# Two seats of experts per round, each expert's weights kept while its blocks last, and tokens' rows scattered to DRAM before the experts run

## The chip, the cores and the metric

One Trainium2 chip, one core of it. The metric is the device time of one execution of the whole program in microseconds (us). The program is a stack of four fp32 layers of a language model for 512 tokens of width 1024. The change touches the mixture of experts of the last two layers.

## The reference

`reference` runs `first_block` (two layers of three mixers) and then `second_block` (two layers, `i` = 0 and 1). Each layer of the second block ends in a mixture of experts:

```python
N_EXPERTS, TOP_E, D_EXPERT = 32, 2, 512

def hier_moe(h, wr_g, br_g, wr_e, br_e, w_gate, w_up, w_down):
    xf = h.reshape(n_tok, d)                     # 512 tokens, d = 1024
    ...                                          # group by softmax, the 2 best experts in it
    gate = (p_top * jax.nn.softmax(e_val, axis=-1)).reshape(-1)
    expert_id = (g_sel * EXPERTS_PER_GROUP + e_sel).reshape(-1)
    ...
    def expert_block(args):
        xb, e = args                             # rows of tokens, their expert
        return (jax.nn.silu(xb @ w_gate[e]) * (xb @ w_up[e])) @ w_down[e]
    ...
    # a token's output is the gate-weighted sum over its two experts

x = x + g2[:, None, :] * hier_moe(h, ...)
```

The inputs are fixed, and so is the routing. Counted from the reference's own router on its own inputs, 1024 assignments fall on the 32 experts like this. Layer 0: experts 26 and 29 get 69 and 135 tokens, all the others between 2 and 61. Layer 1: expert 13 gets 67, all the others between 2 and 61. In blocks of 64 tokens that is 35 blocks in layer 0 (2 for expert 26, 3 for 29, 1 for each other) and 33 in layer 1 (2 for expert 13).

## The kernel before

Everything is fp32. Each layer of the second block ends in three stages, each a block of programs for the engines with a barrier behind it.

**route_and_plan** (`route`, `plan`). The vector engine (DVE) picks the two experts of each token. SyncE (SP) meanwhile issues the weights of experts 0 and 1, six loads. TensorE (PE) ranks each token within its expert by products with triangles and ones (L2569, L2570). DVE lays the work out as items: an item is one expert with up to 64 (`SLOTS`) of its tokens. Items 0 to 31 are the first block of each expert, the items behind them the further blocks. `slot_of` says for each token and item which slot it has, `row_of` where each token's two results will lie, `counts` holds the number of pairs of items and each item's expert. So layer 0 has 35 items in 18 pairs, layer 1 33 in 17.

**items** (`item_experts`). A loop over pairs of items, with a register as its bound. In pair `p` PE does

- gate: 16 products of `hs` with `wg`, two items side by side in the two halves of the array (L2701),
- up: the same with `wu`,
- gather of pair `p + 1` (L2693): `h` times a 0/1 matrix `pick` that DVE has made (L2753), 32 products, which give the turned rows of the next pair's tokens; ScalarE (ACT) copies them to `hs` (L2734) behind it,
- four transposes of `hid` (L2716), a copy to `hidT` on ACT (L2744), and down: 16 products with `wd` (L2701).

DVE multiplies `hid` (L2765) and scales the result `y` (L2772), GpSimd (POOL) stores it (L2678, 128x1024 fp32, 512 KB). SP reloads each of the three pairs of weight tiles as soon as PE is through with it (L2665, L2668, L2671): six loads of 2048 KB per pair, whichever expert stood there before. There is one buffer for each of the weight tiles, so a tile's load for pair `p + 1` lies between its use in `p` and in `p + 1`. In the trace a product of fp32 stands as two instructions.

**moe_residual**. POOL gathers each token's two rows from `expert_rows` by indirect DMA (L2819), DVE adds them to `x`. Rows of `expert_rows` that no token has are never read by a token, but they are cleared once: while the first block's layer 0 does its second attention (`attention` with `cleared_rows`), POOL issues 26 stores of zeros (L647, 13.6 MB). That attention reads its side weights `side_w` through SP's queue (L661). The same attention of the first block's layer 1 clears nothing.

Of the kernel before, what the change touches and what calls it, by code (L numbers as in the profile page):

```python
# [78 lines left out]
class Chip:  # L79
# [8 lines left out]
    def name_tables(self, t):  # L88
# [4 lines left out]
        self.before, self.block_starts, self.numbers, self.number = t["before"], t["block_starts"], t["numbers"], t["number"]  # L93
# [802 lines left out]
def first_layer(chip, l, io, par, row, x, fm, v_first, merged, o_fm, sg, next_norm):  # L896
# [3 lines left out]
    with ExitStack() as ctx:  # L900
# [5 lines left out]
        with ExitStack() as inner:  # L906
            def sbi(name, shape):
# [10 lines left out]
                  side=(fm, gate_jobs(fm, w_in, COL["gb"], sg)), cleared_rows=chip.expert_rows if l == 0 else None)  # L918
# [864 lines left out]
ITEMS = 2 * SEQ // SLOTS + EXPERTS + 4  # L1783
FAR = 16384.0
# [758 lines left out]
def plan(chip, st, choice, routed, routed_ready, slot_of, row_of, counts):  # L2543

# [6 lines left out]
    slot, t3 = st.sb("slot", [P, TILES, E]), st.sb("t3", [P, E, TILES * 2])  # L2551
    blocks, first = st.sb("blocks", [P, E]), st.sb("first", [P, E])
    last = st.sb("last", [P, E])
    slotT = st.sb("slotT", [E, SEQ])
    mine, rowf = st.sb("mine", [P, 2 * TILES, E]), st.sb("rowf", [P, 2 * TILES])
    rangeT, hot = st.sb("rangeT", [E, 2]), st.sb("hot", [E, ITEMS])
    row = st.sb("row", [1, 1 + ITEMS])
    half, over_one = st.sb("half", [1, ITEMS]), st.sb("over_one", [P, TILES, E])
    at_expert, later = st.sb("at_expert", [P, E]), st.sb("later", [E, ITEMS])
# [4 lines left out]
    @st.block.tensor  # L2564
    def _(pe):
        pe.wait_ge(*routed_ready.at(1))
        for t in range(TILES):
            product(pe, B[0][:, t * E:(t + 1) * E], [(chip.before, routed[:, t, :])] +
                    [(chip.ones, routed[:, u, :]) for u in range(t)])  # L2569
        product(pe, B[0][:, TILES * E:(TILES + 1) * E], [(chip.ones, routed[:, u, :]) for u in range(TILES)]  # L2570
                ).then_inc(*ranked.inc())

        pe.wait_ge(*placed.at(1))
        for t in range(TILES):
            pe.transpose(B[1][0:E, t * P:(t + 1) * P], slot[:, t, :], chip.ident)
# [4 lines left out]
        for t in range(TILES):  # L2580
            pe.matmul(B[4][:, t * ITEMS:(t + 1) * ITEMS], slotT[:, t * P:(t + 1) * P], hot[:, :], start=True, stop=True)
        pe.matmul(B[6][0:1, 0:ITEMS], chip.number[0:E, :], hot[:, :], start=True, stop=True).then_inc(*tabled.inc())

    @st.block.vector
    def _(dve):
        link = st.chain(dve, "plan_step")
        dve.wait_ge(*ranked.at(1))

        total = B[0][:, TILES * E:(TILES + 1) * E]
        more = SEQ // SLOTS - 1  # L2590
        link(dve.tensor_tensor(t3[:, :, 0:more], over(total, [P, E, more], 2), over(chip.block_starts[:, 1:], [P, E, more], 1), ALU.is_gt))
        link(dve.tensor_reduce(blocks[:, :], t3[:, :, 0:more], AX.X, ALU.add))
        link(dve.tensor_tensor_scan(last[:, :], chip.ones[:, 0:E], blocks[:, :], 0.0, ALU.mult, ALU.add))
        link(dve.tensor_tensor(first[:, :], last[:, :], blocks[:, :], ALU.subtract))

        ranks = B[0][:, 0:TILES * E].rearrange("p (t e) -> p t e", t=TILES)
        link(dve.tensor_scalar(at_expert[:, :], chip.numbers[:, 0:E], float(SLOTS), None, ALU.mult))
        link(dve.tensor_scalar(blocks[:, :], first[:, :], float(E - 1), float(SLOTS), ALU.add, ALU.mult))
        link(dve.tensor_tensor(blocks[:, :], blocks[:, :], at_expert[:, :], ALU.subtract))
        link(dve.tensor_scalar(over_one[:, :, :], ranks, float(SLOTS), None, ALU.is_ge))  # L2600
        link(dve.tensor_tensor(over_one[:, :, :], over_one[:, :, :], over(blocks[:, :], [P, TILES, E], 1), ALU.mult))
        link(dve.tensor_scalar(slot[:, :, :], routed[:, :, :], 1.0, -FAR, ALU.subtract, ALU.mult))
        link(dve.tensor_tensor(slot[:, :, :], slot[:, :, :], ranks, ALU.add))
        link(dve.tensor_tensor(slot[:, :, :], slot[:, :, :], over(at_expert[:, :], [P, TILES, E], 1), ALU.add))
        dve.tensor_tensor(slot[:, :, :], slot[:, :, :], over_one[:, :, :], ALU.add).then_inc(*placed.inc())

        link(dve.tensor_scalar(half[:, :], chip.numbers[0:1, 0:ITEMS], 2.0, float(E), ALU.mult, ALU.subtract))
        link(dve.tensor_scalar(half[:, :], half[:, :], last[0:1, E - 1:E], None, ALU.is_lt))
# [13 lines left out]
        for n in range(2):
            link(dve.tensor_tensor(mine[:, n * TILES:(n + 1) * TILES, :], choice[:, n], slot[:, :, :], ALU.mult))
        link(dve.tensor_reduce(rowf[:, :], mine[:, :, :], AX.X, ALU.add))
        link(dve.tensor_copy(row_of[:, :], rowf[:, :]))
        link(dve.tensor_copy(row[:, 1:1 + ITEMS], B[6][0:1, 0:ITEMS]))
        link(dve.tensor_copy(counts[:, :], row[:, :]))


def item_experts(chip, i, io, h, slot_of, counts, gate_row, made, weights, weights_loaded):  # L2630

    B = chip.bank
    with chip.stage("items") as st:
        wg, wu, wd = weights
        pick = st.sb("pick", [P, TILES, 2, SLOTS])
        y = st.sb("y", [P, D])
# [9 lines left out]
        picked, gathered, filled = one("picked"), one("gathered"), one("slots_filled")  # L2646
# [484 lines left out]
```

## Time and profile before

| | us |
|---|---|
| median of 3 runs (lowest, highest) | 4123.36 (4121.28, 4138.25) |
| the profiled execution | 4129.7 |
| its span in the trace | 4127.8 |
| items of layer 0, first gate product to end of the last down | 2368.65 to 2915.1 |
| items of layer 1, the same | 3571.02 to 4086.97 |
| PE busy | 3641.8 (88%) |
| DVE, ACT, POOL busy | 1727.8 (42%), 740.4 (18%), 176.1 (4%) |

| slices of 103 us that hold the items | layer 0 (24 to 29) | layer 1 (35 to 40) |
|---|---|---|
| DMA, GB/s | 397 429 429 429 429 153 | 240 430 428 429 429 271 |

The two loops are 1062 us, 26% of the span. A row of the timeline gives the start, the busy time, the engine, the line, the operation with its tiles, how many instructions are merged in the row and, in brackets, how long the engine sat idle before it and what ended that. PE and the DMA queues are both nearly full in the loops, so it has to be read row by row which of them sets the round.

### The profile page before, as it was taken

What the parts mean: (1) busy time and instruction counts of PE and PEld (TensorE: products, weight loads), DVE (VectorE), ACT (ScalarE), POOL (GpSimd) and SP (SyncE); (2) the same over time, 40 slices, a digit from 0 to 9 for tenths busy, and PEclk for the clock granted to TensorE, in tenths of its full rate; (3) what the DMA queues carried; (4) which work ended last, traced back from release to release, by engine and by line L of the source; (5) the groups of instructions that cost most, each with busy time, mean ns of one, the idle gap of its engine ahead of it and who ended that gap; (6) DMA issues with size and microseconds to landing.
All of it is one profiled execution on the core that took longest, in us unless ns stands there. A gap on an engine that the chain in (4) does not pass through costs nothing. (4 is left out here: it accounts for less than half of the span.)

```text
span 4127.8 us, 40648 instructions
## 1 busy us (share of the span) xinstructions
PE 3641.8 (88%) x15948; PEld 1967.4 (48%) x15948; DVE 1727.8 (42%) x3164; ACT 740.4 (18%) x1439; POOL 176.1 (4%) x239
## 2 busy tenths in 40 slices
PE   7998899988899889988889799999589698799995
PEld 4453434884445443388544544444234344554442
DVE  3235556674233554667547310111459626211102
ACT  1132213000113321300011111111231413111111
POOL 0001010001000001000100000000000300000000
PEclk9999999999999999999999799999789899899998
DMA  2215341004121235100512299999450411599996
GB/s 94 74 41 199 124 159 51 1 1 145 51 82 41 67 123 161 51 1 1 183 61 101 122 397 429 429 429 429 153 166 5 122 49 58 240 430 428 429 429 271
DMA packets 200436, 704.48 MB, mean 171 GB/s; under 512 B 21512, under 2 KB 100872, under 8 KB 172656
## 3 DMA queue, kind: packets, MB, share of 16 engines
q1 hardware_dynamic: 174384, 610.25, 38.2%
q0 software_dynamic: 25920, 92.47, 6.3%
q8 instruction: 84, 1.38, 0.1%
q14 instruction: 48, 0.39, 0.0%
HBM read 655.92 MB, written 46.74 MB: 170 GB/s over the span
## 5 line engine op out<-in xcount | busy, mean ns | idle before, releaser
L296 PE MATMUL bank<-fm,w 128*128 128x512 f32 (+1 forms) x1024 | 443.4, 594 | 6.5 <-DMA w<-in_ab_w_in 6.5
L296 PEld LDWEIGHTS bank<-fm,w 128*128 128x128 f32 (+1 forms) x1024 | 191.4, 188 | 256.7 <-issue 248.1
L378 PEld LDWEIGHTS bank<-pick,normed 128*128 128x128 f32 x2368 | 272.2, 195 | 36.1 <-issue 28.4
L2701 PE MATMUL bank<-experts_wd,hidT 128*64 128x512 f32 x1120 | 248.0, 595 | 45.1 <-ACT hidT L2744 45.1
L378 PE MATMUL bank<-pick,normed 128*128 128x128 f32 x2368 | 279.2, 280 | 7.2 <-DVE pick L2753 7.2
L2772 DVE TENSOR_TENSOR y<-bank,mod 128x512 f32<-128x512 f32 x70 | 45.1, 686 | 528.4 <-PE bank L2701 528.4
L676 PE MATMUL bank<-fm,side_w 128*128 128x512 f32 x512 | 251.1, 616 | 6.9 <-DMA side_w<-in_w_in 5.6
L2701 PE MATMUL bank<-experts_wu,hs 128*64 128x512 f32 x1120 | 247.4, 594 | 10.8 <-DMA experts_wu<-in_moe_w_up 10.8
L2701 PE MATMUL bank<-experts_wg,hs 128*64 128x512 f32 x1120 | 246.4, 592 | 2.5 <-ACT hs L2734 2.5
L296 PE MATMUL bank<-w,fm 128*128 128x512 f32 (+1 forms) x512 | 214.8, 582 | 14.8 <-DMA w<-in_w_in 14.8
L296 PE MATMUL bank<-o_fm,w 128*128 128x512 f32 x384 | 181.5, 637 | 47.4 <-DMA w<-in_w_pb 18.9
L2765 DVE TENSOR_TENSOR hid<-bank,act_out 128x512 f32<-128x512 f32 x35 | 37.1, 1059 | 410.0 <-PE bank L2701 410.0
L213 PE MATMUL bank<-w,fm 128*128 128x512 f32 (+1 forms) x448 | 178.8, 559 | 7.1 <-DMA w<-in_cd_w_in 5.8
L378 PE MATMUL bank<-fm,w 128*128 128x512 f32 x384 | 169.4, 597 | 1.4 <-ACT rwkv_a L1297 1.4
L2701 PEld LDWEIGHTS bank<-experts_wd,hidT 128*64 128x64 f32 x1120 | 77.3, 137 | 193.3 <-issue 139.9
L2701 PEld LDWEIGHTS bank<-experts_wu,hs 128*64 128x64 f32 x1120 | 78.5, 137 | 177.7 <-issue 145.4
L296 PEld LDWEIGHTS bank<-w,fm 128*128 128x128 f32 x512 | 99.1, 194 | 129.5 <-issue 114.0
L2701 PEld LDWEIGHTS bank<-experts_wg,hs 128*64 128x64 f32 x1120 | 80.4, 137 | 161.5 <-issue 161.5
L793 ACT ACTIVATE prob<-bank,nmax 128x128 f32<-128x128 f32 (+2 forms) x192 | 111.2, 579 | 210.2 <-DVE nmax L841 146.1
L296 PEld LDWEIGHTS bank<-o_fm,w 128*128 128x128 f32 x384 | 78.3, 206 | 147.5 <-issue 98.0
L2734 ACT ACTIVATE hs<-bank 128x512 f32<-128x512 f32 x74 | 40.2, 594 | 556.9 <-PE bank L378 556.9
L676 PEld LDWEIGHTS bank<-fm,side_w 128*128 128x128 f32 x512 | 91.1, 197 | 90.3 <-issue 83.1
(466 smaller groups left out, 4951.1 us busy)
## 6 DMA issues: line engine op xcount, KB each, us to landing
experts_wg<-in_moe_w_gate SPq DMA_DIRECT2D x70, 2048.0 KB, 15.8
experts_wu<-in_moe_w_up SPq DMA_DIRECT2D x70, 2048.0 KB, 18.3
experts_wd<-in_moe_w_down SPq DMA_DIRECT2D x70, 2048.0 KB, 14.5
ada_w<-in_ada_w POOLq DMA_DIRECT2D x96, 512.0 KB, 4.9
w<-in_w_in SPq DMA_DIRECT2D x48, 512.0 KB, 4.3
w<-in_w_in SPq DMA_DIRECT2D x20, 1024.0 KB, 7.3
expert_rows<-y POOLq DMA_DIRECT2D x35, 512.0 KB, 10.4
side_w<-in_w_in SPq DMA_DIRECT2D x32, 512.0 KB, 3.9
```

Of the source, the lines that this page charges most:

```text
L213: ins = pe.matmul(bank, lhsT, rhs, start=(n == 0), stop=(n == len(todo) - 1))
L296: ins = pe.matmul(bank, lhsT, rhs, start=(n == 0), stop=(n == len(todo) - 1))
L378: last = pe.matmul(out, lhsT, rhs, start=(n == 0), stop=(n == len(pairs) - 1))
L676: last = pe.matmul(SIDE[:, :], side_w[n % 2][:, k_, :], side_h[:, k_, :], start=(k_ == 0), stop=(k_ == DC - 1))
L793: act.activation(prob[s % 4][:, 0:n], S[s % n_scores][:, 0:n], ACT.Exp, bias=nmax[:, s:s + 1], scale=1.0 if bias is None else -1.0, accum_ ...
L2701: ins = pe.matmul(bank[rows, :], lhs[:, k, rows], weights[s][:, k, cols], start=(k == 0), stop=(k == chunks - 1))
L2734: ins = act.activation(hs[:, 4 * n:4 * n + 4, :], B[6 + n][:, :].rearrange("p (k n) -> p k n", k=4), ACT.Copy)
L2765: dve.tensor_tensor(dealt(hid[:, :], FC), B[1][:, :].rearrange("p (q k) -> p q k", k=FC), act_out[:, :].rearrange("p (q k) -> p q k", k=FC ...
L2772: ins = dve.tensor_tensor(y[:, cols], B[4 + d][:, :], gate_row[:, cols], ALU.mult)
```

## The change

- `plan` gives each expert a seat: even experts have seat 0, odd ones seat 1, and each seat takes its experts in order, each for as many rounds as it has blocks (at least one). A round is 64 tokens of seat 0 and 64 of seat 1. The rounds are as many as the fuller seat needs. With the counts above, layer 0 has 18 rounds (17 blocks in seat 0, 18 in seat 1) and layer 1 has 17 (16 and 17).
- SP loads a seat's weights only in a round in which a new expert takes it: a small loop from `FROM_AT` to `TO_AT` around each load. PE waits for a number of landings that it reads from `counts` (`LANDED_AT`). In layer 0 rounds 14, 15, 16 and 17 load one expert each, in layer 1 rounds 7 and 16; round 0 has both from the stage before, all other rounds load two. So 32 experts are loaded per layer instead of 36 and 34.
- The gather products and `pick` are gone. At the end of route_and_plan POOL scatters the rows of `h` to a second DRAM tensor `expert_in` by eight indirect DMAs of 512 KB. SP loads 128 rows of it per round (`xs`, 512 KB), and PE turns them by eight transposes.
- `expert_in` is cleared during the second attention of the first block's layer 0 and `expert_rows` during that of layer 1. Both are 64 * 64 rows, 32 stores of 512 KB, 16.8 MB.

The core of the diff:

```diff
-                  side=(fm, gate_jobs(fm, w_in, COL["gb"], sg)), cleared_rows=chip.expert_rows if l == 0 else None)
+                  side=(fm, gate_jobs(fm, w_in, COL["gb"], sg)), cleared_rows=(chip.expert_in, chip.expert_rows)[l])
...
+        link(dve.tensor_scalar(blocks[:, :], blocks[:, :], 1.0, None, ALU.max))
+        for seat in range(2):
+            link(dve.tensor_tensor_scan(last[:, seat::2], chip.ones[:, 0:E // 2], blocks[:, seat::2], 0.0, ALU.mult, ALU.add))
+        dve.tensor_tensor(first[:, :], last[:, :], blocks[:, :], ALU.subtract).then_inc(*placed.inc())
...
+        dve.tensor_copy(row_of[:, :], rowf[:, :]).then_inc(*rows_placed.inc())
...
+            def load_rows(q):
+                sp.dma_start(xs[:, :], h_rows[bass.ds(q * P, P), :]).then_inc(*rows_loaded.inc(16))
+
+            def load(name, w, free, loaded, p, seats):
...
+                with sp.Fori(*seats) as s:
+                    e = sp.value_load(counts[0:1, bass.ds(p * 2 + s + EXPERT_AT, 1)], min_val=0, max_val=EXPERTS - 1)
+                    sp.wait_ge(*free.at(p + 1))
...
+            sp.wait_ge(*h_rows_written)
+            load_rows(0)
+            sp.wait_ge(*gathered.at(1))
+            load_rows(1)
+            n = rounds_of(sp)
             with sp.Fori(1, n) as p:
...
+                load("moe_w_gate", wg, gate_done, gate_loaded, p, seats)
+                load("moe_w_up", wu, up_done, up_loaded, p, seats)
+                sp.wait_ge(*gathered.at(p + 1))
+                load_rows(p + 1)
+                load("moe_w_down", wd, down_done, down_loaded, p, seats)
...
-            def gather(q):
-
-                pe.wait_ge(*picked.at(q + 1))
+            def turn(q):
+
+                pe.wait_ge(*rows_loaded.at(16 * q + 16))
                 pe.wait_ge(*filled.at(q + 1))
                 for k in range(DC):
-                    ins = product(pe, B[6 + k // 4][:, (k % 4) * P:(k % 4 + 1) * P],
-                                  [(h[:, t, k * P:(k + 1) * P], pick[:, t, :, :].rearrange("p a s -> p (a s)")) for t in range(TILES)])
+                    ins = pe.transpose(B[6 + k // 4][:, (k % 4) * P:(k % 4 + 1) * P], xs[:, k * P:(k + 1) * P], chip.ident)
...
+                landed = pe.value_load(counts[0:1, bass.ds(p + LANDED_AT, 1)], min_val=16, max_val=32 * ROUNDS)
...
-                pe.wait_ge(*gate_loaded.at(32 * p + 32))
+                pe.wait_ge(*gate_loaded.at(landed))
...
+                    pool.wait_ge(*rows_placed.at(1))
+                    for at in range(2 * TILES):
+                        pool.indirect_dma_start(out=h_rows, out_offset=bass.IndirectOffsetOnAxis(ap=row_of[:, at:at + 1], axis=0),
+                                                in_=h[:, at % TILES, :], in_offset=None).then_inc(*written.inc(16))
```

PE in the loop of layer 0, before: from the gather of pair 0 to the end of the loop's body.

```order
L378 MATMUL bank<-pick,normed 128x128 x32
...
L2708 ISA
L2701 MATMUL bank<-experts_wg_0,hs 64x512 x16
L2701 MATMUL bank<-experts_wu_0,hs 64x512 x16
L378 MATMUL bank<-pick,normed 128x128 x32
L2714 REGISTER_ALU
L2716 MATMUL bank<-consts,hid 128x128 x4
L2701 MATMUL bank<-experts_wd_0,hidT 64x512 x16
```

The same place now:

```order
L2700 MATMUL bank<-consts,xs 128x128 x8
...
L2713 TENSOR_LOAD experts_counts
...
L2708 MATMUL bank<-experts_wg,hs 64x512 x16
L2708 MATMUL bank<-experts_wu,hs 64x512 x16
L2697 ISA
L2700 MATMUL bank<-consts,xs 128x128 x8
L2724 MATMUL bank<-consts,hid 128x128 x4
L2708 MATMUL bank<-experts_wd,hidT 64x512 x16
```

Eight transposes stand where the 32 products of the gather stood, and a load of a register from `counts` stands at the top of each round.

SP in the body of the same loop, before:

```order
L2661 TENSOR_LOAD experts_counts
...
L2665 DMA experts_wg_0<-in_moe_w_gate 128x4096
...
L2665 DMA experts_wg_0<-in_moe_w_gate 128x4096
L2668 DMA experts_wu_0<-in_moe_w_up 128x4096 x2
L2671 DMA experts_wd_0<-in_moe_w_down 128x4096 x2
```

And now (the first row stands ahead of the loop):

```order
L2656 DMA xs<-expert_in 128x1024 x2
...
L2662 TENSOR_LOAD experts_counts
...
L2664 DMA experts_wg<-in_moe_w_gate 128x4096
...
L2661 COMPARE_AND_BRANCH
...
L2664 DMA experts_wu<-in_moe_w_up 128x4096
...
L2656 DMA xs<-expert_in 128x1024
...
L2664 DMA experts_wd<-in_moe_w_down 128x4096
```

Each weight load stands once, in a loop of its own with a register load and a branch, and the load of the next round's rows stands between up and down.

POOL around the items of layer 0 now; ahead of the loop there was nothing in route_and_plan before.

```order
L2807 DMA expert_in<-normed,experts_row_of 4096x1024 x8
L117 UNCONDITIONAL_BRANCH
L2681 UNCONDITIONAL_BRANCH
L2651 TENSOR_LOAD experts_counts
...
L2686 DMA expert_rows<-y 128x1024
```

The eight scattering DMAs are new; behind them POOL's loop has its store of `y` as before.

## Rows read from the trace of the kernel before

**Rows 1.** The page, GB/s that the DMA moved, in 40 slices.
```profile
GB/s 94 74 41 199 124 159 51 1 1 145 51 82 41 67 123 161 51 1 1 183 61 101 122 397 429 429 429 429 153 166 5 122 49 58 240 430 428 429 429 271
```

**Rows 2.** Timeline of PE, an early round of layer 0.
```profile
2398.60 7.04 PE L2701 MATMUL bank<-experts_wg,hs 128*64 128x512 f32 x32
...
2412.43 7.41 PE L378 MATMUL bank<-pick,normed 128*128 128x128 f32 x64
...
2421.57 7.09 PE L2701 MATMUL bank<-experts_wd,hidT 128*64 128x512 f32 x32 [1.29 <-ACT hidT L2744]
2428.49 7.04 PE L2701 MATMUL bank<-experts_wg,hs 128*64 128x512 f32 x32
```

**Rows 3.** Timeline of PE, the last round of layer 0.
```profile
2891.86 7.09 PE L2701 MATMUL bank<-experts_wu,hs 128*64 128x512 f32 x32 [0.46 <-DMA experts_wu<-in_moe_w_up]
...
2908.01 7.09 PE L2701 MATMUL bank<-experts_wd,hidT 128*64 128x512 f32 x32 [1.29 <-ACT hidT L2744]
```

**Rows 4.** Ten late rounds: length, busy PE, PEld, DVE, ACT, POOL, PEclk, DMA share, GB/s.
```profile
2585.90:2891.70 305.80, 288.19 (x1640) 143.27 (x1640) 31.08 (x50) 34.70 (x51) 5.31 (x10) 1.00 1.01 429
```

**Rows 5.** DMA issues of the whole program: count, KB each, median us to landing.
```profile
experts_wg<-in_moe_w_gate SPq DMA_DIRECT2D x70, 2048.0 KB, 15.8
...
ada_w<-in_ada_w POOLq DMA_DIRECT2D x96, 512.0 KB, 4.9
...
out<-rows SPq DMA_DIRECT2D x4, 512.0 KB, 2.6
```

**Rows 6.** Timeline, the start of the items of layer 0: SP's last weights, then PE.
```profile
2330.94 0.96 SPq L2800 DMA_DIRECT2D experts_wd<-in_moe_w_down  x2
...
2357.08 10.31 PE L378 MATMUL bank<-pick,normed 128*128 128x128 f32 x64 [3.62 <-DVE pick L2753]
...
2368.65 7.09 PE L2701 MATMUL bank<-experts_wg,hs 128*64 128x512 f32 x32 [1.26 <-ACT hs L2734]
...
2375.57 7.04 PE L2701 MATMUL bank<-experts_wu,hs 128*64 128x512 f32 x32
```

**Rows 7.** Timeline of PE, layer 1: first up, last down.
```profile
3577.94 7.04 PE L2701 MATMUL bank<-experts_wu,hs 128*64 128x512 f32 x32
...
4079.88 7.09 PE L2701 MATMUL bank<-experts_wd,hidT 128*64 128x512 f32 x32 [1.29 <-ACT hidT L2744]
```

**Rows 8.** The tile experts_wd, 2325 to 2370 us: its two loads.
```profile
DMA to landing us min/median/max: 27.1/29.3/31.5
```

**Rows 9.** Timeline of POOL, one of eight indirect DMAs in moe_residual.
```profile
4095.81 0.97 POOL L2819 DMA_INDIRECT rows<-expert_rows,experts_row_of  x1 [0.30 <-issue]
```

**Rows 10.** Timeline, ACT's copies behind a gather, and eight transposes on PE elsewhere.
```profile
2875.81 1.09 ACT L2734 ACTIVATE hs<-bank 128x512 f32<-128x512 f32 x2 [14.34 <-PE bank L378]
2876.78 0.60 ACT L2744 ACTIVATE hidT<-bank 128x512 f32<-128x512 f32 x1
...
2936.19 1.97 PE L512 MATMUL bank<-consts,xn 128*128 128x128 f32 x8 [21.10 <-DVE xn L500]
```

**Rows 11.** Timeline, the second attention of the first block's layers 0 and 1.
```profile
365.42 77.54 SPq L661 DMA_DIRECT2D side_w<-in_w_in  x8
...
394.46 3.78 PE L676 MATMUL bank<-fm,side_w 128*128 128x512 f32 x4 [5.56 <-DMA side_w<-in_w_in]
...
475.38 0.56 SPq L1175 DMA_DIRECT2D rwkv_wup<-in_rwkv_w_up  x1
...
1403.20 70.41 SPq L661 DMA_DIRECT2D side_w<-in_w_in  x8
...
1506.04 0.49 SPq L1175 DMA_DIRECT2D rwkv_wup<-in_rwkv_w_up  x1
```

**Rows 12.** The tile side_w, 360 to 480 us (layer 0): its eight loads.
```profile
DMA to landing us min/median/max: 3.8/4.9/17.8
```

**Rows 13.** Timeline of PE in layer 1 of the second block: bursts behind short idle times.
```profile
3432.89 1.12 PE L711 MATMUL bank<-consts,prob 128*128 128x128 f32 x4 [2.23 <-DVE prob L855]
...
3460.14 3.70 PE L2418 MATMUL bank<-out_w,attn_y 128*128 128x512 f32 x8 [3.14 <-DMA out_w<-in_cd_w_out]
```

More of the change, by code:

```diff
@@ L2540, in _, with plan @@
         dve.tensor_tensor(routed[:, :, :], choice[:, 0], choice[:, 1], ALU.add).then_inc(*routed_ready.inc())
-def plan(chip, st, choice, routed, routed_ready, slot_of, row_of, counts):
+def plan(chip, st, choice, routed, routed_ready, row_of, rows_placed, counts):
     E = EXPERTS
[L2551 to L2559, printed above, removed]
+    t3, past = st.sb("t3", [P, E, SEQ // SLOTS]), st.sb("past", [P, 2 * TILES, SEQ // SLOTS - 1])
+    blocks, first, last = st.sb("blocks", [P, E]), st.sb("first", [P, E]), st.sb("last", [P, E])
+    mine, rank, rowf = st.sb("mine", [P, 4, TILES, E]), st.sb("rank", [P, 4 * TILES]), st.sb("rowf", [P, 2 * TILES])
+    span, hot, new = st.sb("span", [E, 2]), st.sb("hot", [E, ITEMS]), st.sb("new", [E, ITEMS])
+    row = st.sb("row", [1, N_COUNTS])
     ranked, placed, turned, taken = st.count("ranked"), st.count("placed"), st.count("turned"), st.count("hot_ready")
@@ L2579, in _ @@
         pe.wait_ge(*taken.at(1))
-        for t in range(TILES):
-            pe.matmul(B[4][:, t * ITEMS:(t + 1) * ITEMS], slotT[:, t * P:(t + 1) * P], hot[:, :], start=True, stop=True)
-        pe.matmul(B[6][0:1, 0:ITEMS], chip.number[0:E, :], hot[:, :], start=True, stop=True).then_inc(*tabled.inc())
+        pe.matmul(B[6][0:1, 0:ITEMS], chip.number[0:E, :], hot[:, :], start=True, stop=True)
+        pe.matmul(B[6][0:1, ITEMS:2 * ITEMS], chip.ones[0:E, 0:1], new[:, :], start=True, stop=True).then_inc(*tabled.inc())
     @st.block.vector
@@ L2589, in _ @@
         total = B[0][:, TILES * E:(TILES + 1) * E]
[L2590 to L2596, printed above, removed]
@@ L2622, in _ @@
[L2622 to L2626, printed above, removed]
+        n = SEQ // SLOTS
+        link(dve.tensor_tensor(t3[:, :, :], over(total, [P, E, n], 2), over(chip.block_starts, [P, E, n], 1), ALU.is_gt))
+        link(dve.tensor_reduce(blocks[:, :], t3[:, :, :], AX.X, ALU.add))
@@ new lines, in _ @@
+        dve.wait_ge(*turned.at(1))
+        for n in range(2):
+            link(dve.tensor_copy(span[:, n:n + 1], B[3][0:E, n * P:n * P + 1]))
+        own = chip.own_round[0:E, :]
+        link(dve.tensor_scalar(new[:, :], own, span[:, 0:1], None, ALU.is_equal))
+        link(dve.tensor_scalar(hot[:, :], own, span[:, 0:1], None, ALU.is_ge))
+        dve.scalar_tensor_tensor(hot[:, :], own, span[:, 1:2], hot[:, :], ALU.is_lt, ALU.mult).then_inc(*taken.inc())
+        link(dve.tensor_tensor(row[:, N_AT:N_AT + 1], last[0:1, E - 1:E], last[0:1, E - 2:E - 1], ALU.max))
@@ new lines, in _ @@
+        dve.wait_ge(*tabled.at(1))
+        link(dve.tensor_copy(row[:, EXPERT_AT:EXPERT_AT + ITEMS], B[6][0:1, 0:ITEMS]))
+        begun = B[6][0:1, ITEMS:2 * ITEMS]
+        start, end, landed = (row[:, at:at + ROUNDS] for at in (FROM_AT, TO_AT, LANDED_AT))
+        link(dve.tensor_scalar(end, begun[:, 1::2], 1.0, None, ALU.add))
+        link(dve.tensor_scalar(start, begun[:, 0::2], -1.0, 1.0, ALU.mult, ALU.add))
+        link(dve.scalar_tensor_tensor(start, end, 1.0, start, ALU.subtract, ALU.min))
@@ L2627, in _, with item_experts @@
+        link(dve.tensor_tensor(t3[0:1, 0:ROUNDS, 0], end, start, ALU.subtract))
+        link(dve.tensor_tensor_scan(landed, chip.ones[0:1, 0:ROUNDS], t3[0:1, 0:ROUNDS, 0], 0.0, ALU.mult, ALU.add))
+        link(dve.tensor_scalar(landed, landed, 16.0, None, ALU.mult))
         link(dve.tensor_copy(counts[:, :], row[:, :]))
-def item_experts(chip, i, io, h, slot_of, counts, gate_row, made, weights, weights_loaded):
+def item_experts(chip, i, io, counts, gate_row, h_rows, h_rows_written, made, weights, weights_loaded):
@@ L2788, in sbi @@
                 return items.enter_context(chip.nc.sbuf_tensor(f"experts_{name}_{i}", shape, dt))
[L2789 to L2790 removed]
+            counts = sbi("counts", [1, N_COUNTS], I32)
+            weights = [sbi(n, shape) for n, shape in (("wg", [P, 2, DC, D_EXP]), ("wu", [P, 2, DC, D_EXP]), ("wd", [P, 2, FC, D]))]
+            h_rows, written = chip.expert_in, chip.rows_spread
             with chip.stage("route_and_plan") as st:
```

129 lines of the change are left out of this document (53 added, 76 removed).

## The prediction, made before the run

> **What bounds the kernel now.** I read the slices first, then the timeline of TensorE (PE) through both loops over items. The slices show 429 GB/s through both loops [rows 1], so the DMA is a candidate. The timeline says when it decides. In an early round one gate product starts at 2398.60 and the next at 2428.49, 29.9 us, and in between PE never waits for a DMA: gate 6.9, up 6.9, gather 7.25, four short transposes, 1.29 of waiting for the copy to `hidT`, down 6.9 [rows 2]. So the first rounds belong to PE. In late rounds up waits 0.46 us for its weights [rows 3], ten rounds take 305.8 us, and the DMA share is 1.01 [rows 4]. That is 30.6 us per round, and it is the DMA's: six loads of 2048 KB (2.10 MB each) and the store of `y` (0.52 MB) are 13.11 MB, and 13.11 / 0.429 = 30.6. The two limits lie 0.7 us apart. A change that frees only one of them gains next to nothing.
>
> **Rounds after the change.** DMA: a full round loads the same 12.58 MB, stores 0.52 MB and now also loads 0.52 MB of `xs`: 13.63 MB, 31.8 us, 1.2 more than before. A round with one new expert moves 7.34 MB, 17.1 us. PE: the gather goes. From its start to down it took 2421.57 - 2412.43 = 9.1 us [rows 2]. Now come eight transposes; cold they take 1.97 us, so about 1.0 at full clock [rows 10]. Behind them stand ACT's two copies to `hs` and the one to `hidT`, 1.6 us in a row [rows 10], with about 0.2 of handing over. That is 2.8 instead of 9.1, so a PE round is 29.9 - 6.3 = 23.6 us. Full rounds are thus the DMA's (31.8), and PE's gain of 6.3 us buys nothing there. Four one-load rounds in a row at the end of layer 0 are PE's (23.6, not 17.1). So is the last round of layer 1. Round 7 of layer 1 stands alone among full rounds, and PE's lag of some 14 us behind the DMA is made up in round 8, so it costs the DMA's 17.1.
>
> SP's new loops put a register load and a branch before each issue. Before, each load was issued with some 10 us of others still queued (the median gate load lands 15.8 us after its issue, and two of them are only 9.8 us of data [rows 5]). I cost them at nothing for that cover. The load of `xs` sits between up and down on SP and waits for a turn done a round earlier, so nothing queues behind it. PE's register load for `landed` is bounded by 0 and by the 1.26 us at the loop's entry which hid such a load before [rows 6]. It counts only in the five PE rounds; I take 0 and keep 6 for the range.
>
> **Loop of layer 0**, from the end of gate(0), when the DMA restarts. Before: 2908.01 + 7.09 - 2375.57 = 539.5 us [rows 3, 6]. After: 13 full rounds of 13.63 MB are 413.2 us, about 4 for first latencies, the last full down 6.9, four PE rounds 94.4: 518.5. Gain 21.0. **Loop of layer 1.** Before 4079.88 + 7.09 - 3577.94 = 509.0 [rows 7]. After: 14 full rounds and round 7, 198.2 MB, 462.1 us, then 4, 6.9 and one PE round of 23.6: 496.6. Gain 12.4. The six expert loads that vanish are 37.7 MB, 88 us of DMA; the 35 loads of `xs` and PE's rounds take most of that back.
>
> **The start of each loop.** Before, gate(0) started 11.6 us after the gather did and ended at 2375.57 [rows 6]. Now a chain stands there. The first six weights are all landed at about 2331.4 + 31.5 = 2362.9 [rows 6, 8]. The scatter is 4.19 MB more on the same engines, 9.8 us at 429 GB/s. Its issue takes 8 x 1.27 = 10.2 us [rows 9]. Even if it began only where the gather began (2357.1; the new plan has the rows several us earlier) it would be issued by 2367.3, so bandwidth ends it: 2372.7. Then the load of `xs`, 512 KB: between 2.6 (`out`) and 4.9 us (`ada_w`) [rows 5], I take 3.5. Then transposes at half clock 1.97 [rows 10], the copy and hand-over 1.26, and gate(0) itself. PE has idled before it and starts it at half clock: the first gather took 10.31 us, a later one 7.41, 2.9 for warming up [rows 2, 6]. So gate(0) ends at 2372.7 + 3.5 + 2.0 + 1.3 + 9.8 = 2389.2, 13.6 us later than before. Layer 1 has the same chain. Cost 27.2. From both sides: if the scatter lands with the weights it is 3.8 per layer; if it is held up as the worst `side_w` load was, by 17.8 - 4.9 = 12.9 [rows 12], it is 26.5.
>
> **Clearing.** The trace holds its price. Layer 0's attention with the zeros behind it takes 475.38 - 365.42 = 110.0 us, layer 1's without them 102.8 [rows 11]. The 7.1 between them is one wait of 5.56 for a side weight that stood beside the stores, and slow products behind it (four in 3.78 us) [rows 11]. Now layer 1 pays 7.1 too. Both clear longer, in layer 0 16.8 MB instead of 13.6, 7.5 us more of a full DMA, and the fourth side load lands inside it. That costs 0 to another 5.6 in each; I take 2.5 each. Cost 12.1, between 0 (hidden by another order of waits) and 18.
>
> **Sum.** +27.2 - 21.0 - 12.4 + 12.1 = +5.9 us. On the profiled execution that is 4129.7 + 5.9 = 4135.6. It stood 6.3 above the median, so against the median 4123.4 I expect 4129.3.
>
> **Rivals.** (1) *The scatter hides.* Its rows go through at the weights' cost and it lands with the last of them, while gate(0) needs only the first. For: the gate weights are first in the queue. Against: the weights alone keep the engines busy until 2362.9 [rows 6, 8], and a side load beside POOL's stores took 17.8 us, so one queue can starve beside another [rows 12]. Time: -19.6, 4110.
> (2) *PE's clock becomes the bound (slower).* In full rounds PE now idles 31.8 - 23.6 = 8.2 us, in three gaps of 2 to 3 us ahead of up, down and gate. Behind an idle time of 2.23 us four transposes took 1.12 us, 0.28 each, as slow as the cold ones (1.97 / 8); behind 3.14 us eight products took 3.70, 0.46 each, against 0.95 for the cold ones of the attention [rows 10, 11, 13]. So a short gap makes the clock fall from 2.4 to 1.2 GHz sometimes and sometimes not. One fall costs 2.9 us. One or two per round vanish in the 8.2; three are 8.7, 0.5 more than it holds. This rival decides from three falls in every round: 27 full rounds x 0.5 = 13.5, and a fall in each of the five PE rounds 14.5, so +28: 4157. The Trainium skill ("TensorE: Matmul & The Clock Gate", section "HAM oscillation — how this bites in real kernels") holds that a loop whose compute per tile is shorter than its DMA wait falls cold at each tile. By that every gap falls and the sum is this rival's; the two rows disagree with each other on it, so it has a chance and no more.
> (3) *The scatter is held up*, +12.9 per layer, 4155.
> (4) *The vanished loads show in full*, one-load rounds at 17.1 us: five x 6.5 = 32.5 faster, 4097. Against it stand three products of 6.9 us per round, 20.8 already.
>
> **Numbers.** Forecast 0.55 (own range 4118 to 4143: clearing, `xs` and the register loads at their ends), (1) 0.15, (2) 0.14, (3) 0.11, (4) 0.05. About 0.5%, 21 us, is what a measurement can tell from no change: faster is below 4103, slower above 4144. Faster: (4) and the low end of (1), 0.07. Slower: most of (2) and (3), the top of the forecast, 0.25. The range reaches from the lower part of (1), 4106, to the upper part of (2) and (3), 4160.
>
> **What the profile will show.** 35 rounds and 64 loads of each weight tensor. Full rounds of 31.8 us, with waits for DMA ahead of up, down and gate, and the DMA share at 1.0; a period over 32.5 with PE always busy would be (2). One-load rounds at the end of layer 0 of 23.6 with no DMA wait; 17 would be (4). gate(0) ends 57.8 us after the last weights' issue, with the wait for `xs` before it; under 50 is (1), over 67 is (3). A wait for `side_w` in both second attentions. Wrong altogether: a DMA that goes idle between loads (SP's loops), or another count of rounds.

## The result, and the profile after

The changed kernel takes 4139.36 us (median of 20 runs, 4132.06 to 4147.43), the kernel before 4125.66 (20 runs on the same chip, 4119.38 to 4138.25). The ratio is 1.0032 with a 95% interval of 1.0026 to 1.0037, so 11 to 15 us slower. The profiled executions are 4139.43 and 4129.7 us, their spans 4137.7 and 4127.8.

The page of the kernel after: span, PE, GB/s in 40 slices [against rows 1], and the issues (count, KB each, median us to landing).

```profile
span 4137.7 us, 37995 instructions
...
PE 3479.2 (84%) x13856; PEld 1754.2 (42%) x13857; DVE 1698.3 (41%) x3088; ACT 740.8 (18%) x1439; POOL 212.6 (5%) x294
...
GB/s 98 70 41 224 133 154 51 1 1 145 51 81 41 211 135 167 51 1 1 174 53 117 158 354 429 428 428 349 138 161 0 126 44 58 262 429 420 426 428 266
...
experts_wg<-in_moe_w_gate SPq DMA_DIRECT2D x64, 2048.0 KB, 19.5
...
xs<-expert_in SPq DMA_DIRECT2D x37, 512.0 KB, 21.4
```

PE is busy 163 us less than before (3641.8), and the kernel is slower all the same. The slices say why: in the loops the DMA still moves 428 or 429 GB/s (layer 1 has one slice of 420 and one of 426). In slice 14 (layer 1's second attention) 67 GB/s have become 211, which is the new clearing.

A full round is one in which both seats load a new expert, a one-load round one in which a single seat does. The windows of the kernel after: eight full rounds, then three one-load rounds, of layer 0 (columns as in rows 4).

```profile
2550.90:2805.60 254.70, 197.92 (x864) 71.39 (x864) 18.78 (x24) 27.64 (x40) 4.26 (x8) 0.93 1.01 428
2830.92:2901.63 70.71, 67.51 (x326) 24.26 (x324) 7.04 (x9) 10.37 (x15) 1.60 (x3) 1.00 0.85 311
```

A full round takes 254.70 / 8 = 31.84 us at a DMA share of 1.01 (before 30.58 [rows 4]), a one-load round 70.71 / 3 = 23.57 us with PE busy throughout. The timeline of PE, a full round:

```profile
2582.72 9.60 PE L2708 MATMUL bank<-experts_wu,hs 128*64 128x512 f32 x32 [3.81 <-DMA experts_wu<-in_moe_w_up]
...
2595.07 7.09 PE L2708 MATMUL bank<-experts_wd,hidT 128*64 128x512 f32 x32 [0.93 <-ACT hidT L2752]
2603.67 7.09 PE L2708 MATMUL bank<-experts_wg,hs 128*64 128x512 f32 x32 [1.51 <-DMA experts_wg<-in_moe_w_gate]
2614.57 8.78 PE L2708 MATMUL bank<-experts_wu,hs 128*64 128x512 f32 x32 [3.82 <-DMA experts_wu<-in_moe_w_up]
```

PE waits for the DMA 3.8 us ahead of up and 1.5 ahead of gate, where in such a round before it waited 0.46 in all [rows 3]. Here is the gather's saving: it became waiting. Up took 9.60 and 8.78 us instead of 7.09: behind the longer wait a part of its products ran at 1.2 GHz instead of 2.4 (granted clock 0.50 in the first 3.3 us of the first of them; 0.93 on the mean of the window, before 1.00), and yet the next up came 31.85 us after this one.

The timeline of the kernel after, the start of layer 0's loop [against rows 6 and 9]:

```profile
2338.36 0.82 SPq L2797 DMA_DIRECT2D experts_wg<-in_moe_w_gate  x2
...
2340.41 0.98 SPq L2797 DMA_DIRECT2D experts_wd<-in_moe_w_down  x2
...
2347.20 6.18 PE L379 MATMUL bank<-routed,consts 128*128 128x32 f32 x28 [9.43 <-DVE routed L2543]
...
2358.45 1.05 POOL L2807 DMA_INDIRECT expert_in<-normed,experts_row_of  x1 [271.92 <-DVE experts_row_of L2604]
...
2367.39 0.95 POOL L2807 DMA_INDIRECT expert_in<-normed,experts_row_of  x1 [0.31 <-issue]
...
2382.84 5.70 SPq L2656 DMA_DIRECT2D xs<-expert_in  x2
...
2386.20 1.97 PE L2700 MATMUL bank<-consts,xs 128*128 128x128 f32 x8 [26.31 <-DMA xs<-expert_in]
...
2389.34 9.01 PE L2708 MATMUL bank<-experts_wg,hs 128*64 128x512 f32 x32 [1.17 <-ACT hs L2742]
...
2398.18 7.03 PE L2708 MATMUL bank<-experts_wu,hs 128*64 128x512 f32 x32
```

The last of eight scatters is issued at 2367.39, but SP, which waits for all of them, issues the rows' load at 2382.84. PE waits 26.3 us there. Two windows of that stretch:

```profile
2375.00:2380.00 5.00, 0.00 (x0) 0.00 (x0) 0.00 (x0) 0.00 (x0) 0.00 (x0) 0.50 1.02 418
2380.00:2386.00 6.00, 0.00 (x0) 0.00 (x0) 0.00 (x0) 0.00 (x0) 0.00 (x0) 0.50 0.33 109
```

Until 2380 the DMA engines are full (418 GB/s), behind it nearly idle: the scatter ends when all that was queued is through, 12.58 MB of weights and 4.19 MB of rows. The weights are ahead of it: the two `wd` loads landed 27.0 and 33.5 us behind their issue, the later one at about 2374 and only 2.0 us later than before (31.5 [rows 8]).

The timeline of the kernel after, the second attention of the first block's layers 0 and 1 [against rows 11], and of the tile `side_w` in layer 1:

```profile
364.79 24.72 SPq L662 DMA_DIRECT2D side_w<-in_w_in  x4
...
475.58 0.57 SPq L1176 DMA_DIRECT2D rwkv_wup<-in_rwkv_w_up  x1
...
1402.63 24.75 SPq L662 DMA_DIRECT2D side_w<-in_w_in  x4
...
1433.15 3.78 PE L677 MATMUL bank<-fm,side_w 128*128 128x512 f32 x4 [5.16 <-DMA side_w<-in_w_in]
...
1513.24 0.48 SPq L1176 DMA_DIRECT2D rwkv_wup<-in_rwkv_w_up  x1
```

```profile
DMA to landing us min/median/max: 3.8/5.5/17.1
```

From `side_w` to `rwkv_wup` it is 110.8 us in layer 0 (before 110.0) and 110.6 in layer 1 (before 102.8).

| where, by the two profiles | us |
|---|---|
| start of the loops, from the routing's products to the end of gate(0): 37.9 to 51.0, and 37.0 to 49.7 | +13.1, +12.7 |
| loop of layer 0, from there to the end of the last down: 539.5 to 520.3 | -19.2 |
| loop of layer 1: 509.0 to 500.3 | -8.7 |
| the two second attentions | +0.8, +7.8 |
| the rest, from front to back: to the attention of layer 0 -0.6, to that of layer 1 -0.8, to the first routing +2.3, between the loops +2.6, behind them 0 | +3.5 |
| sum | +10.0 (spans: +9.9) |

### The profile page after: what moved, and what is told of

Same layout as the page of the kernel before. It is cut to its first block and busy times, and to the rows that moved or that the text cites. A ratio compares the mean times of both kernels' runs of the same rounds, so it can differ in the third digit from the quotient of the medians.

```text
span 4137.7 us, 37995 instructions
## 1 busy us (share of the span) xinstructions
PE 3479.2 (84%) x13856; PEld 1754.2 (42%) x13857; DVE 1698.3 (41%) x3088; ACT 740.8 (18%) x1439; POOL 212.6 (5%) x294
## 5 line engine op out<-in xcount | busy, mean ns | idle before, releaser
L2708 PE MATMUL bank<-experts_wu,hs 128*64 128x512 f32 x1120 | 279.0, 656 | 79.8 <-DMA experts_wu<-in_moe_w_up 79.8
L2708 PE MATMUL bank<-experts_wg,hs 128*64 128x512 f32 x1120 | 264.0, 626 | 49.4 <-DMA experts_wg<-in_moe_w_gate 47.1
L2708 PE MATMUL bank<-experts_wd,hidT 128*64 128x512 f32 x1120 | 258.0, 615 | 49.4 <-issue 27.1
L297 PE MATMUL bank<-o_fm,w 128*128 128x512 f32 x384 | 179.9, 632 | 48.1 <-DMA w<-in_w_pb 19.2
L2708 PEld LDWEIGHTS bank<-experts_wg,hs 128*64 128x64 f32 x1120 | 92.5, 144 | 218.4 <-issue 215.2
L297 PEld LDWEIGHTS bank<-w,fm 128*128 128x128 f32 x512 | 99.2, 194 | 129.0 <-issue 114.0
L214 PEld LDWEIGHTS bank<-w,fm 128*128 128x128 f32 x448 | 83.5, 199 | 103.4 <-issue 96.9
L1877 DVE SCALAR_TENSOR_TENSOR ada_sums<-ada_w,cond,ada_sums 128x1024 f32<-128x1024 f32 x84 | 105.6, 1282 | 31.9 <-DMA ada_w<-in_ada_w 31.1
```

The source lines that it names most:

```text
L214: ins = pe.matmul(bank, lhsT, rhs, start=(n == 0), stop=(n == len(todo) - 1))
L297: ins = pe.matmul(bank, lhsT, rhs, start=(n == 0), stop=(n == len(todo) - 1))
L1877: ins = dve.scalar_tensor_tensor(sums, self.slot[n % self.slots][:, :], by, sums, ALU.mult, ALU.add)
L2708: ins = pe.matmul(bank[rows, :], lhs[:, k, rows], weights[:, s, k, cols], start=(k == 0), stop=(k == chunks - 1))
```

## Experiments

Each was compared with the kernel before on its own chip (medians 4124.5, 4125.1 and 4125.2 there). Their ratios can be set against 1.0032. Differences from the changed kernel are those of the medians, taken on different chips. By the ratios down_late is 16 us below it (17 by the medians), core_clear 12 (15.7), no_row_loads 40 (39), best 30 (32), always_load 57 above it (57) and busy_pe 41 (44), so the two bases differ by up to 3.3 us.

**down_late**: the first round's `wd` loads are issued behind the first load of rows, not before the scatter.

```diff
-                    for name, pair, loaded in zip(("moe_w_gate", "moe_w_up", "moe_w_down"), weights, weights_loaded):
+                    for name, pair, loaded in zip(("moe_w_gate", "moe_w_up"), weights, weights_loaded):
...
             load_rows(0)
+            for s in range(2):
+                sp.dma_start(wd[:, s], io["moe_w_down"][i, s].rearrange("(p k) n -> p k n", p=P)).then_inc(*down_loaded.inc(16))
```

> The changed kernel, but SP issues the first two experts' down weights only behind the first load of xs, not with the gate and up weights ahead of the scatter. Theory (the start is bandwidth: the scatter lands last because 12.6 MB of weights share the engines with it): with 4.2 MB less ahead of it the scatter is bound by its issue, xs lands about 10 us earlier, gate(0) of both layers ends about 10 us earlier, and the down weights land in the idle time that follows. Median about 20 us below the changed kernel, near 4119. Rival (the start is a chain of issues and landings, whatever else is on the engines): under 3 us per layer, 4134 or more.

Measured: 4122.24 us, ratio 0.9993 (0.9983 to 1.0002), so 17 us less than the changed kernel. The timeline of its start:

```profile
2348.07 6.18 PE L379 MATMUL bank<-routed,consts 128*128 128x32 f32 x28 [9.43 <-DVE routed L2543]
...
2368.28 0.95 POOL L2809 DMA_INDIRECT expert_in<-normed,experts_row_of  x1 [0.30 <-issue]
...
2373.54 0.34 SPq L2656 DMA_DIRECT2D xs<-expert_in  x1
2373.93 0.90 SPq L2670 DMA_DIRECT2D experts_wd<-in_moe_w_down  x2
...
2376.93 1.97 PE L2702 MATMUL bank<-consts,xs 128*128 128x128 f32 x8 [16.16 <-DMA xs<-expert_in]
...
2388.90 7.03 PE L2710 MATMUL bank<-experts_wu,hs 128*64 128x512 f32 x32
```

With 4.19 MB less in front, the scatter lands 5.3 us behind its last issue instead of 15.4, and from the routing's products to the end of gate(0) it is 40.8 us instead of 51.0, in layer 1 41.8 instead of 49.7. That is 18 us for both. The scatter waits for the weights' bytes, and a start that was only a chain of issues and landings would have stayed where it was.

**core_clear**: both clearings stand in the scan of the first block's layers, in POOL's program, instead of beside the second attention.

```diff
-                  side=(fm, gate_jobs(fm, w_in, COL["gb"], sg)), cleared_rows=(chip.expert_in, chip.expert_rows)[l])
+                  side=(fm, gate_jobs(fm, w_in, COL["gb"], sg)), cleared_rows=None)
...
+                    pool.memset(zero[:, :], 0.0).then_inc(*zero_made.inc())
+                    pool.wait_ge(*zero_made.at(1))
+                    for rows_ in ((chip.expert_in, chip.expert_rows)[l],):
+                        for n in range(rows_.shape[0] // P):
+                            pool.dma_start(rows_[n * P:(n + 1) * P, :], zero[:, :]).then_inc(*wiped.inc(16))
+                    pool.wait_ge(*wiped.at(wiped.total))
```

> The changed kernel, with both clearings moved out of the two second attentions into the scans of the same layers, where the trace shows DMA at 1 GB/s. Theory (clearing costs through the side weights that stand beside its stores): both attentions take 102.8 us again instead of 110.6 to 110.8, nothing appears in the scans, 15.6 us less, near 4124. Rival (each store costs wherever it stands, or the 7 us come from something else in layer 0): the time moves by under 5 us.

Measured: 4123.66 us, ratio 1.0002 (0.9991 to 1.0013), 15.7 us less by the medians. The stretch of the attention is 102.9 us in layer 0 and 103.0 in layer 1, its ends in layer 1:

```profile
1391.03 1.01 SPq L662 DMA_DIRECT2D side_w<-in_w_in  x2
...
1494.03 0.48 SPq L1176 DMA_DIRECT2D rwkv_wup<-in_rwkv_w_up  x1
```

So each clearing beside an attention costs 7.6 to 7.9 us, and beside the scan nothing that can be seen. **before_core_clear** makes the same edit in the kernel before (one clearing, 26 stores).

> The kernel before, with only its clearing of expert_rows (26 stores of zeros) moved from the second attention to the scan of the first block's layer 0. My theory (clearing beside an attention costs that attention 7 to 8 us, because its side weights load slowly meanwhile; beside the scan it costs nothing): the stage from SP's first side load to its first load of the next stage falls from 110.0 to 103 us, the whole to about 4118 us, 0.9983 of the kernel before. Rival (the seated kernel gained from the move for a reason of its own, such as the two clearings of it): no change, 4125 us.

Measured: 4118.92 us, ratio 0.9985 (0.9976 to 0.9994), so 6.3 us less than the kernel before, and the stretch in layer 0 fell from 110.0 to 102.7 us. The price was there before the change, which doubled it.

**always_load**: each round loads both seats' weights, whether a new expert takes the seat or not. That is the scatter and the turned rows without the saved weights.

```diff
-        link(dve.tensor_scalar(end, begun[:, 1::2], 1.0, None, ALU.add))
-        link(dve.tensor_scalar(start, begun[:, 0::2], -1.0, 1.0, ALU.mult, ALU.add))
-        link(dve.scalar_tensor_tensor(start, end, 1.0, start, ALU.subtract, ALU.min))
+        link(dve.tensor_scalar(end, begun[:, 1::2], 0.0, 2.0, ALU.mult, ALU.add))
+        link(dve.tensor_scalar(start, begun[:, 0::2], 0.0, None, ALU.mult))
```

> The changed kernel, with SP loading both seats' experts in every round, also where the expert is the one that stands there (in the rounds in which a seat has run out, expert 0). Theory: the five rounds that PE sets at 23.6 us and the lone one-load round of layer 1 (17.1 us of DMA) become DMA rounds of 31.8: 5 x 8.2 + 14.7 = 56 us more, near 4195. That is what keeping the weights is worth. Rival (the kept weights are hidden anyway, and freeing PE from the gather is what the changed loops gain): under 20 us more.

Measured: 4196.37 us, ratio 1.0169 (1.0152 to 1.0186), 57 us more than the changed kernel. Its window over ten rounds, through what were one-load rounds:

```profile
2578.15:2896.57 318.42, 246.14 (x1081) 89.71 (x1081) 23.48 (x30) 34.55 (x50) 5.31 (x10) 0.95 1.01 428
```

All rounds take 31.84 us. The saved loads are worth 57 us to this kernel, and still it doesn't reach the kernel before: without them the scatter, the loads of rows and the second clearing together cost 72.

**seats_gather**: the other half alone. Seats and saved loads, but the rows gathered by PE from `pick` as before, no scatter, one clearing. The slots are made from `row_of` on DVE:

```diff
-        dve.tensor_copy(row_of[:, :], rowf[:, :]).then_inc(*rows_placed.inc())
+        link(dve.tensor_copy(row_of[:, :], rowf[:, :]))
+        link(dve.scalar_tensor_tensor(slots2[:, :, :], over(numbers[:, 0:ITEMS], shape, 1), -float(SLOTS),
+                                      over(rowf[:, :], shape, 2), ALU.mult, ALU.add))
...
-                    ins = pe.transpose(B[6 + k // 4][:, (k % 4) * P:(k % 4 + 1) * P], xs[:, k * P:(k + 1) * P], chip.ident)
+                    ins = product(pe, B[6 + k // 4][:, (k % 4) * P:(k % 4 + 1) * P],
+                                  [(h[:, t, k * P:(k + 1) * P], pick[:, t, :, :].rearrange("p a s -> p (a s)")) for t in range(TILES)])
```

> The seats alone: each expert's weights load once, but the rows of tokens are gathered by TensorE's products as in the kernel before (a slot table made from row_of, pick on DVE, 32 products), nothing is scattered, and only expert_rows is cleared, once, beside the second attention of the first block's layer 0. My theory (the seats' rounds with one load gain only down to what PE needs for a round, 29.9 us with the gather and 23.6 us without it; the start and the clearing lose because of the scatter): the loops lose 0.7 us in each of 6 rounds with one load, the start is as before, so about 4125 - 4 = 4121 us, 0.999 of the kernel before, and gate(0) begins about 13 us earlier behind the routing than in the changed kernel. Rival A (fewer bytes of weights gain by themselves: 24 MB less at 0.429 MB/us for a pair of experts in 6 rounds, 14.6 us each at most): towards 4070 us. Rival B (the start's loss belongs to the seats' longer plan on DVE and not to the scatter): the start stays late by some 10 us a layer, about 4141 us.

Measured: 4122.93 us, ratio 0.9996 (0.9986 to 1.0006). Its timeline of PE, the start and two one-load rounds:

```profile
2336.02 6.18 PE L379 MATMUL bank<-routed,consts 128*128 128x32 f32 x28 [9.43 <-DVE routed L2543]
...
2365.14 7.09 PE L2709 MATMUL bank<-experts_wg,hs 128*64 128x512 f32 x32 [1.17 <-ACT hs L2743]
2372.06 7.04 PE L2709 MATMUL bank<-experts_wu,hs 128*64 128x512 f32 x32
...
2819.30 7.04 PE L2709 MATMUL bank<-experts_wg,hs 128*64 128x512 f32 x32
...
2849.19 7.04 PE L2709 MATMUL bank<-experts_wg,hs 128*64 128x512 f32 x32
```

gate(0) ends 36.0 us behind the start of the routing's products (before 37.9, after 51.0): the new plan on DVE costs nothing that can be seen, the scatter is the late start. One-load rounds last 29.89 us, PE's round with the gather. The 4 us that were forecast from them are too few for this measurement, whose interval includes no change. So neither half helps by itself in a way that can be seen: without the scatter PE holds the one-load rounds, without the seats the DMA holds all of them.

**no_row_loads**: the rows of round 2 and later are not loaded, so PE turns the rows of round 1 in their place; the rest is as in the changed kernel.

```diff
-                sp.wait_ge(*gathered.at(p + 1))
-                load_rows(p + 1)
...
-                pe.wait_ge(*rows_loaded.at(16 * q + 16))
+                pe.wait_ge(*rows_loaded.at(16 if isinstance(q, int) else 32))
```

> The changed kernel without the loads of the rows of rounds 2 and later: PE turns the rows of round 1 in all of them, so the output is not the reference's. It still loads all weights. My theory (a round with two experts lasts as long as the DMA engines need for its bytes): 0.5 MB less of 13.6 MB takes 1.2 us off each of 27 such rounds, period 31.8 to 30.6 us, in all about -33 us, 4106 us. Rival (such a round is held by PE, or by SP's issues, and not by the bytes): the period stays at 31.8 us, 4139 us. Second rival (small loads of 512 B to 4 KB per row cost the queues more than their bytes): the period falls by over 2 us, below 4085 us.

Measured: 4100.63 us, ratio 0.9936 (0.9920 to 0.9951), 39 us less (27 full rounds at 1.27 are 34; the other 5 are not accounted for). Its window over eight full rounds:

```profile
2545.47:2790.02 244.55, 202.71 (x864) 70.69 (x864) 18.79 (x24) 27.64 (x40) 4.26 (x8) 0.90 1.01 429
```

That is 30.57 us per round, 1.27 less: 0.52 MB at 0.429 MB/us are 1.22. The round is the DMA's bytes. The granted clock in the window is even lower (0.90), though PE idles less in all (41.8 us of the window, against 56.8 in the changed kernel): in each of these rounds it waits 3.5 to 3.8 us ahead of up, and up then takes 8.4 to 10.1 us. The rounds are shorter all the same.

**busy_pe**: PE turns the rows seven times in the loop, so it waits less and works longer.

```diff
-                for k in range(DC):
+                for k in (k for _ in range(1 if isinstance(q, int) else 7) for k in range(DC)):
```

> The changed kernel, with PE doing the eight transposes of each round in the loop seven times over, about 6 us more of PE work per round, as much as the gather took before. Theory (the DMA sets the full rounds, PE's falls to the lower clock are hidden there): full rounds stay at 31.8 us and the clock stays high in them; only the five PE rounds grow, by 6 us each, and the one-load round of layer 1 a little, 31 to 38 us in all, near 4173. Rival (falls of the clock hold up the full rounds): they get shorter by 0.5 us or more each, so less than 20 us in all.

Measured: 4183.34 us, ratio 1.0131 (1.0114 to 1.0147), 44 us more. Its windows over seven full rounds and over three one-load rounds:

```profile
2520.24:2743.64 223.40, 197.60 (x1092) 93.62 (x1092) 16.51 (x21) 24.18 (x35) 3.73 (x7) 0.98 1.01 428
2837.71:2924.14 86.43, 82.57 (x471) 40.02 (x469) 7.08 (x9) 10.36 (x15) 1.60 (x3) 1.00 0.70 254
```

Full rounds stay at 31.91 us, one-load rounds go from 23.57 to 28.81. 5.2 us of extra work cost next to nothing in 27 rounds and their full length in the one-load rounds of layer 0. By first and last up, the loops lost 21.8 and 9.4 us, and behind each stands the last round's extra turning, 5.2 more: 41.6 of the 44.

**best**: down_late and core_clear together.

> The two edits that were tried apart, together: the loads of wd of the first round are issued behind the first load of the rows, and both clearings stand in the scan of the first block's layers instead of in the second attention. My theory (the late start and the clearing are two separate losses in different stages, so they add): -17 us of the one and -15.7 us of the other against 4139.4, so about 4106.5 us, 0.9955 of the kernel before, and below both kernels. Rival (both edits move the same loss, the load on the DMA engines that something later has to pay): the gain of one alone, 4122 us.

Measured: 4107.01 us (4098.53 to 4113.6, five runs), ratio 0.9960 (0.9946 to 0.9973). That is below both kernels, 32 us under the changed one (17.1 and 15.7 are 32.8, by the ratios 16 and 12 against 30: the two add up) and 18 under the kernel before. Against the kernel before with its clearing moved too (4118.92) the seats, the scatter and the later `wd` are worth 12 us.

## Why the prediction was right, and where its terms were off

It said 4129.3 with a range of 4106 to 4160, and with 0.07 for faster and 0.25 for slower it left 0.68 for a change of less than 0.5%. Measured are 4139.36 and +0.32%, in the likeliest of its cases and inside that one's own range (4118 to 4143). The limits of the rounds, the late start and the price of the clearing came out by the mechanisms that it names. The size did not: it forecast +5.9 us, and by the medians the change is +13.7. Nor was 0.5% the least that could be told apart: with 20 runs each the interval is 0.26 to 0.37%.

- **Full rounds, 31.8 us, the DMA's.** Measured 31.84. no_row_loads takes bytes away and the period follows; busy_pe adds work to PE and it does not. Shown.
- **One-load rounds, 23.6 us, PE's.** Measured 23.57, with no wait for a DMA. Shown by busy_pe, and by seats_gather from the other side (29.89, predicted 29.9 for PE with the gather). That 29.89 is also the round of the kernel before [rows 2], which has no load of `landed`, so the register load on PE costs nothing that can be seen. A slip without weight: 37 loads of `xs` stand in the trace and not 35, as each loop also loads the rows of one round past its last.
- **Loop of layer 0, -21.0.** Measured -19.2: 520.3 us instead of 518.5; the 1.8 were not followed up. **Loop of layer 1, -12.4.** Measured -8.7. The term that was too small is round 7. The prediction let PE's lag be "made up in round 8", so that it costs the DMA's 17.1 us. Its up products:

```profile
3780.19 9.90 PE L2708 MATMUL bank<-experts_wu,hs 128*64 128x512 f32 x32 [3.83 <-DMA experts_wu<-in_moe_w_up]
3806.62 7.04 PE L2708 MATMUL bank<-experts_wu,hs 128*64 128x512 f32 x32
3830.66 7.09 PE L2708 MATMUL bank<-experts_wu,hs 128*64 128x512 f32 x32 [0.30 <-DMA experts_wu<-in_moe_w_up]
3863.56 8.78 PE L2708 MATMUL bank<-experts_wu,hs 128*64 128x512 f32 x32 [3.84 <-DMA experts_wu<-in_moe_w_up]
```

  The three periods around it are 83.4 us, so the one-load round cost 83.4 - 2 x 31.84 = 19.7 us, 2.6 more. Its 34.6 MB moved at 415 GB/s instead of 428. Two windows in which PE works off its lag:

```profile
3800.00:3815.00 15.00, 14.86 (x74) 5.35 (x71) 2.32 (x3) 0.82 (x2) 0.53 (x1) 1.00 1.00 369
3815.00:3830.00 15.00, 14.07 (x68) 4.75 (x67) 1.29 (x2) 2.64 (x4) 0.53 (x1) 1.00 0.99 411
```

  PE frees the tiles late there: from 3800.15 to 3807.01 SP issued one load of `wd` and nothing else. That fewer loads in flight are why fewer bytes moved is argued and not shown, since the DMA's busy share stays at 1.00. The other 1 us of the loop is not accounted for.
- **Start of the loops, +13.6 each.** Measured 13.1 and 12.7. gate(0) ends 57.8 us (2398.18 - 2340.41) after the first of the two last weight loads was issued. The forecast of 57.8 counted from the second, about half a microsecond later, so the measured value for it is 57.3. The mechanism (the weights' bytes go first, and bandwidth ends the scatter) is shown by down_late. Rival (1), the scatter that lands with the last weights, is out: they landed at about 2374, and SP issued the load of rows at 2382.84. So is (3), the one that is held up.
- **Clearing, 7.1 in layer 1 and 2.5 more in each.** Measured 7.8 and 0.8 for the two layers, 8.6 instead of 12.1. The 2.5 us more in each were too many, and their lower bound of 0 was nearer: the longer stores of zeros catch no further side load. Of the 7.8 us in layer 1 the one wait of 5.16 us and the slow products behind it (3.78 us for four that take 1.88 a little later) are 7.1.
- **The clock, rival (2).** PE's clock did fall in full rounds: the granted clock of the window is 0.93 where it was 1.00, and up takes 8.78 or 9.60 us behind a wait of 3.8. But there were none, one or two falls per round and not three, and they lie in waiting time. A fall also cost less than the 2.9 us of the forecast: gate, up or down took 8.4 to 9.9 us instead of 7.09. The Trainium skill ("TensorE: Matmul & The Clock Gate", section "HAM oscillation — how this bites in real kernels") describes a loop whose compute per tile is shorter than its DMA wait, and there every tile starts cold and pays for it. The prediction read that as a fall at every gap here. By the page's own condition this loop is another case, since its groups of products last 7 us and its waits at most 3.9. The trace has falls behind some of the waits only. On the price in full rounds the runs decide: no_row_loads has a lower clock yet (0.90) and shorter rounds, and busy_pe has a higher one (0.98) and rounds no shorter. In the full rounds the DMA is what the round waits for, and the falls cost nothing that can be seen. In the one-load rounds of layer 0 there were none (granted clock 1.00), so what they would cost there isn't shown.
- **The rest.** By the profiles these four terms make +6.5 us where the prediction has +5.9. That they agree so well is luck: the loops gained 5.5 us less than forecast, and the starts and the clearing cost 4.9 less. What it lacked are two things of another kind, which with the 0.6 make up the 7.8 us between +5.9 and +13.7. The rest of the program took 3.5 us longer. And the profile of before lay above its median (by 4.0 us of the 20 runs), that of after at its median: the prediction carried that offset over to both.

Why the rest is 3.5 us longer stays open. One stretch that shows such scatter is a block of attention between the two loops (`bias_scratch` loads to the next weights), which the change doesn't touch. Its windows in the kernel before, in the changed kernel and in busy_pe:

```profile
3208.80:3289.00 80.20, 61.57 (x352) 33.20 (x352) 58.41 (x140) 43.48 (x101) 38.94 (x16) 0.89 0.42 106
```

```profile
3211.70:3295.50 83.80, 63.10 (x352) 33.79 (x352) 57.85 (x140) 43.54 (x101) 38.72 (x16) 0.87 0.38 101
```

```profile
3240.11:3331.06 90.95, 67.08 (x352) 35.78 (x352) 57.91 (x140) 43.54 (x101) 38.71 (x16) 0.83 0.35 93
```

The same 352 products take 80 to 91 us, at a granted clock of 0.89 down to 0.83. In seats_gather, best, core_clear and before_core_clear it was 78.5 to 80.8, in down_late 84.3, in always_load 86.5, in no_row_loads 90.95. Each is one execution, so whether the kernel or chance decides it isn't shown. Differences of 10 us between single executions mean little here; it is medians of several runs that separate the kernels.

## What to carry to other kernels

When two engines set a loop's round within a few per cent of each other, count what a change takes from and gives to each: here the weights' saving was cashed only in the rounds with little DMA, the gather's only there too, and neither half was worth anything that could be measured alone. A scatter to DRAM that the next stage reads back costs the bytes of everything that is queued in front of it, so issue only what is needed earlier, and the rest behind the read. Bulk stores that "have time" can still take it from small loads that someone waits for, as they did here; put them where nobody loads.

## What the runs showed of the hardware

- A scatter issued late on POOL's queue, behind 12.58 MB of weights on SP's, was through when all of it was through (15.4 us after its last issue; with 8.39 MB in front 5.3). Being on a queue of its own did not let it pass: the last weights landed only 2.0 us later than without it.
- 428 to 429 GB/s were held in the full rounds, whatever the mix of 2 MB loads, 512 KB loads and stores; and their period followed from the bytes to within 0.1 us (30.58, 31.84 and 30.57 us for 13.11, 13.63 and 13.11 MB). Around the single one-load round of layer 1 it was 415 GB/s.
- SP's inner loops with a register load ahead of each issue, and PE's register load for `landed`, cost nothing that can be seen: the DMA share stayed at 1.01 in full rounds, and PE's round with the gather is 29.89 us with the register load (seats_gather) and without it (before).
- Behind waits of 3.8 us PE's up product took 7.09, 8.41, 8.78 or 9.6 to 9.9 us in one and the same loop body.
